# Expert weights of a routed layer streamed in chunks of 2 MB through eight slots, in place of 4 MB through four

## The reference, cut to what matters

```
# hierarchical_moe: h [256, 1024]; 8 groups of 8 experts, FF = 512
g_w, g_idx = top_k(softmax(h @ w_group + b_group), 1)
e_w, e_idx = top_k(softmax(logits of the chosen group), 2)      # weights normalised, times g_w
for each token and each of its two experts e:
    hid = silu(h @ w1[e]) * (h @ w3[e])                         # [512]
    y  += weight * (hid @ w2[e])                                # [1024]
x = x + y
```

## Time and profile before

| | |
|---|---|
| median of 3 runs | 1761.36 us (1760.98 to 1761.41) |
| the profiled execution | 1762.46 us, span 1760.6 us |
| TensorE matmul busy | 1384.9 us (79%) |
| VectorE, ScalarE busy | 19%, 12% |
| DMA queue of SyncE | 503.69 MB, 24080 packets |
| stage of the experts | about 440 to 1348 us of the span |

### The profile page before, as it was taken

The page is one execution under the profiler, slowest core; times in us unless marked ns, Lnnn a source line. Parts: engine busy times, 40 slices in busy tenths (PEclk is TensorE's granted clock), DMA queues, the critical chain, the costliest instruction groups (busy, mean ns, idle before and its releaser), DMA issues.

```text
span 1760.6 us, 16409 instructions
## 1 busy us (share of the span) xinstructions
PE 1384.9 (79%) x7184; PEld 778.7 (44%) x7184; DVE 329.5 (19%) x585; ACT 209.0 (12%) x366; POOL 1.4 (0%) x6
## 2 busy tenths in 40 slices
PE   6999989888866676656666666666667999999996
PEld 5756886775322122212221222122214546788882
DVE  2233432312211001101010101010101221252221
ACT  1000032202000000000000000000001001143300
POOL 0000000000000000000000000000000000000000
PEclk9999998988987788878887888888878999999998
DMA  7324133317999999999999999999997433332310
GB/s 285 114 103 172 67 117 146 102 51 330 394 429 433 433 431 429 433 434 432 429 430 435 433 429 430 435 433 430 430 435 337 171 134 137 132 144 108 142 50 24
DMA packets 24550, 504.43 MB, mean 287 GB/s; under 512 B 4672, under 2 KB 4928, under 8 KB 6336
## 3 DMA queue, kind: packets, MB, share of 16 engines
q1 hardware_dynamic: 24080, 503.69, 68.6%
q10 hardware_dynamic: 432, 0.17, 0.0%
HBM read 502.81 MB, written 1.05 MB: 286 GB/s over the span
## 4 chain that ended last, share of the span: by engine, by line
PE 51%; DMA 44%; DVE 3%; ACT 1%; issue 1%; SPq 0%; DVEq 0%; ACTq 0%
DMA arena<-in_experts 44%; PE psP L803 35%; PE psP L481 5%; PE psP L492 3%; DVE arena L1298 2%; PE psB L1064 1%; PE psB L793 1%; PE psA L948 1%; PE psB L948 1%; PE psA L1030 1%; PE psA L1029 1%; PE psA L793 0%; PE psA L502 0%; PE psP L848 0%; PE psP L842 0%
## 5 line engine op out<-in xcount | busy, mean ns | idle before, releaser
L803 PE MATMUL psP<-arena,ring 128*128 128x256 f32 x1664 | 369.3, 384 | 2.2 <-DVE arena L1298 1.4
L803 PEld LDWEIGHTS psP<-arena,ring 128*128 128x128 f32 x1664 | 319.1, 193 | 48.1 <-issue 4.2
L481 PE MATMUL psP<-ring,arena 128*32 128x512 f32 x1024 | 162.1, 792 | 103.9 <-DMA ring<-in_experts 103.9
L803 PE MATMUL psP<-ring,arena 128*128 128x512 f32 (+2 forms) x576 | 233.1, 564 | 7.3 <-DVE arena L1298 7.3
L481 PE MATMUL psP<-arena 128*32 128x512 f32 x1024 | 158.1, 774 | 99.8 <-DMA arena<-in_experts 99.8
L1298 DVE TENSOR_TENSOR X<-X,psA 128x512 f32<-128x512 f32 x68 | 46.8, 688 | 682.1 <-PE psA L502 682.1
L803 PEld LDWEIGHTS psP<-ring,arena 128*128 128x128 f32 x576 | 105.7, 191 | 126.1 <-issue 126.0
L481 PEld LDWEIGHTS psP<-ring,arena 128*32 128x32 f32 x1024 | 41.0, 139 | 223.2 <-issue 176.5
L481 PEld LDWEIGHTS psP<-arena 128*32 128x32 f32 x1024 | 37.3, 136 | 217.9 <-DMA arena<-in_experts 126.5
L492 PE MATMUL psP<-arena 128*32 128x512 f32 x512 | 76.8, 754 | 53.6 <-DMA arena<-in_experts 49.8
L492 PE MATMUL psP<-ring,arena 128*32 128x512 f32 x512 | 73.4, 725 | 48.0 <-DMA ring<-in_experts 44.5
(11 more groups left out here) (223 smaller groups left out, 748.3 us busy)
## 6 DMA issues: line engine op xcount, KB each, us to landing
arena<-in_experts SPq DMA_DIRECT2D x48, 4096.0 KB, 33.3
ring<-in_experts SPq DMA_DIRECT2D x48, 4096.0 KB, 33.3
ring<-in_u_gl SPq DMA_DIRECT2D x6, 2048.0 KB, 7.7
ring<-in_u_hf SPq DMA_DIRECT2D x2, 2048.0 KB, 11.9
ring<-in_u_hq SPq DMA_DIRECT2D x2, 2048.0 KB, 22.0
ring<-in_u_hv SPq DMA_DIRECT2D x2, 2048.0 KB, 7.7
ring<-in_u_hg SPq DMA_DIRECT2D x2, 2048.0 KB, 7.4
ring<-in_u_ga SPq DMA_DIRECT2D x2, 2048.0 KB, 7.5
```

Source lines behind the costliest of these rows:

```text
L481: mm = pe.matmul(z[j * CAP:(j + 1) * CAP, :], x[:, 4 * half + k, j * CAP:(j + 1) * CAP], held[c % 4][:, j, k * 512:(k + 1) * 512], start=( ...
L803: mm = pe.matmul(dst, lhs_of(o, k), rhs_of(o, k), start=(k == 0), stop=(k == kc - 1))
```

## The change

Chunks are halved: 12 a group, each of 2 MB, each partition's row 16 KB, and eight places in `held`. `used` counts 12 a group. The order in which the first eight places are filled follows a list of their own: after the step wa1 has been read out (areas 8 and 9), after the third product with v (areas 2 and 3), after wb0 (ring slot 3), wb1 (areas 4 and 5, ring slot 0), wo0 (slot 1) and wo1 (slot 2, areas 6 and 7). `wrow` no longer waits for wb1 but for vm1, an earlier step. `up` takes the quarters it is to work as arguments and waits for each; the number and the order of the products, the scatters and the gathers stay as they were. The waits of the second layer's first four units are adapted to the new places.

```diff
-CHUNKS_G = [("w1", 0), ("w1", 1), ("w3", 0), ("w3", 1), ("w2", 0), ("w2", 1)]
+CHUNKS_G = [(w, q) for w in ("w1", "w3", "w2") for q in range(4)]
 NC_G = len(CHUNKS_G)
+HELD = 8
...
-        held = [area(2, EG, 2048), ring[:, 0:2, :].rearrange("p a (h n) -> p (a h) n", h=2),
-                ring[:, 2:4, :].rearrange("p a (h n) -> p (a h) n", h=2), area(6, EG, 2048)]
+        held = [area(8, EG, 1024), area(2, EG, 1024), ring[:, 3, :].rearrange("p (h n) -> p h n", h=EG), area(4, EG, 1024),
+                ring[:, 0, :].rearrange("p (h n) -> p h n", h=EG), ring[:, 1, :].rearrange("p (h n) -> p h n", h=EG),
+                ring[:, 2, :].rearrange("p (h n) -> p h n", h=EG), area(6, EG, 1024)]
...
-            def up(pair, c, z, x, half):
-
-                wait_chunk(pair, c)
-                for k in range(4):
-                    for j in range(EG):
-                        mm = pe.matmul(z[j * CAP:(j + 1) * CAP, :], x[:, 4 * half + k, j * CAP:(j + 1) * CAP],
-                                       held[c % 4][:, j, k * 512:(k + 1) * 512],
-                                       start=(half == 0 and k == 0), stop=(half == 1 and k == 3))
-                mm.then_inc(used, 1)
+            def up(pair, c, z, x, *parts):
+
+                for q in parts:
+                    wait_chunk(pair, c + q)
+                    for k in range(2):
+                        for j in range(EG):
+                            mm = pe.matmul(z[j * CAP:(j + 1) * CAP, :], x[:, 2 * q + k, j * CAP:(j + 1) * CAP],
+                                           held[(c + q) % HELD][:, j, k * 512:(k + 1) * 512],
+                                           start=(q == 0 and k == 0), stop=(q == 3 and k == 1))
+                    mm.then_inc(used, 1)
...
-            wait_full(sp, ("proj", "wb1"))
+            wait_full(sp, ("proj", "vm1"))
             sp.dma_start(wrow, ins["final_norm_w"].unsqueeze(0).broadcast_to([P, D])).then_inc(row_in, 16)
...
-            before_chunk = [("proj", "wb1"), ("proj", "wo0"), ("proj", "wo1"), ("proj", "wo1")]
+            freed_by = [(empty, "wa1"), (full, "pv"), (full, "wb0"), (full, "wb1"), (full, "wb1"), (full, "wo0"), (full, "wo1"),
+                        (full, "wo1")]
...
-                        sp.wait_ge(used, r * (GROUPS * NC_G) + q * (2 * NC_G) + (c - 3))
+                        sp.wait_ge(used, r * (GROUPS * NC_G) + q * (2 * NC_G) + (c - (HELD - 1)))
...
-                    sp.wait_ge(used, rounds * (GROUPS * NC_G) - (2 if n < 2 else 1))
+                    sp.wait_ge(used, rounds * (GROUPS * NC_G) - (3, 2, 1, 5)[n])
...
-    stream = np.empty((GROUPS, NC_G, P, EG, 2048), np.float32)
+    stream = np.empty((GROUPS, NC_G, P, EG, 1024), np.float32)
```

More of the change, by code:

```diff
@@ L383, in build @@
         rounds_ready = sem("rounds_ready")
-        chunk_in = [sem(f"chunk_in_{i}") for i in range(4)]
+        chunk_in = [sem(f"chunk_in_{i}") for i in range(HELD)]
         used = sem("used")
@@ L452, in chunk_of @@
         def chunk_of(c):
-            return held[c % 4], chunk_in[c % 4]
+            return held[c % HELD], chunk_in[c % HELD]
         SCATTER = [(0, 0, 0), (0, 1, 512), (1, 0, 0), (1, 1, 512)]
@@ L472, in wait_chunk, with down @@
             def wait_chunk(pair, c):
-                pe.wait_ge(chunk_in[c % 4], pair * 48 + 16 * (c // 4 + 1))
-            def up(pair, c, z, x, half):
-                wait_chunk(pair, c)
-                for k in range(4):
-                    for j in range(EG):
-                        mm = pe.matmul(z[j * CAP:(j + 1) * CAP, :], x[:, 4 * half + k, j * CAP:(j + 1) * CAP],
-                                       held[c % 4][:, j, k * 512:(k + 1) * 512],
-                                       start=(half == 0 and k == 0), stop=(half == 1 and k == 3))
-                mm.then_inc(used, 1)
-            def down(pair, c, half):
-                wait_chunk(pair, c)
-                for f in range(2):
+                pe.wait_ge(chunk_in[c % HELD], pair * 48 + 16 * (c // HELD + 1))
+            def up(pair, c, z, x, *parts):
[7 more added lines that the diff above has]
+                    mm.then_inc(used, 1)
+            def down(pair, c):
+                for f in range(4):
+                    wait_chunk(pair, c + f)
                     for cols in range(2):
@@ L492, in down @@
                             mm = pe.matmul(zY[j * CAP:(j + 1) * CAP, cols * 512:(cols + 1) * 512],
[L493 to L496, removed]
+                                           hidT[:, f, j * CAP:(j + 1) * CAP],
+                                           held[(c + f) % HELD][:, j, cols * 512:(cols + 1) * 512],
+                                           start=(f == 0), stop=(f == 3))
+                    mm.then_inc(used, 1)
             def scatter(parts):
@@ L522, in moe_tensor @@
                         pe.wait_ge(gate_read, it + 1)
-                        up(pair, c, zG, xs[u], 0)
+                        up(pair, c, zG, xs[u], 0, 1)
                         pe.wait_ge(xs_ready, it * 2 + 2)
@@ L528, in moe_tensor @@
                         scatter((0, 1))
-                        up(pair, c + 1, zG, xs[u], 1)
+                        up(pair, c, zG, xs[u], 2, 3)
                         pe.wait_ge(hid_ready, it + 1)
-                        up(pair, c + 2, zU, xs[u], 0)
+                        up(pair, c + 4, zU, xs[u], 0, 1)
                         pe.wait_ge(added, it * 4 + 2)
                         scatter((2, 3))
-                        up(pair, c + 3, zU, xs[u], 1)
+                        up(pair, c + 4, zU, xs[u], 2, 3)
                         pe.wait_ge(sel_ready, it + 2)
@@ L548, in moe_tensor @@
                         pe.wait_ge(hidT_ready, it + 1)
-                        down(pair, c + 4, 0)
-                        down(pair, c + 5, 1)
+                        down(pair, c + 8)
             last = pe.snap(rounds * GROUPS)
@@ L567, in moe_scalar @@
                     it = act.snap(r * GROUPS + g)
-                    act.wait_ge(used, it * NC_G + 2)
+                    act.wait_ge(used, it * NC_G + 4)
                     act.wait_ge(hid_ready, it + 1)
@@ L575, in moe_scalar @@
                     act.activation(hidT.rearrange("p f n -> p (f n)"), ps["B"][:, 0:512], ACT.Copy).then_inc(hidT_ready, 1)
-                    act.wait_ge(used, it * NC_G + 6)
+                    act.wait_ge(used, it * NC_G + 12)
                     act.wait_ge(scattered, it * 4 + 4)
@@ L695, in experts @@
                         add(it, 2, 3)
-                        dve.wait_ge(used, it * NC_G + 4)
+                        dve.wait_ge(used, it * NC_G + 8)
                         dve.wait_ge(gate_read, it + 2)
@@ L738, in _ @@
             sp.dma_start(rtw[:, :, 8:72], ins["router_expert_w"][0].rearrange("(k p) n -> p k n", p=P)).then_inc(rt_in, 16)
-            wait_full(sp, ("proj", "wb1"))
+            wait_full(sp, ("proj", "vm1"))
             sp.dma_start(wrow, ins["final_norm_w"].unsqueeze(0).broadcast_to([P, D])).then_inc(row_in, 16)
-            before_chunk = [("proj", "wb1"), ("proj", "wo0"), ("proj", "wo1"), ("proj", "wo1")]
+            freed_by = [(empty, "wa1"), (full, "pv"), (full, "wb0"), (full, "wb1"), (full, "wb1"), (full, "wo0"), (full, "wo1"),
+                        (full, "wo1")]
             def pair_loads(r, q, peeled):
                 for c in range(2 * NC_G):
-                    if peeled and c < 4:
-                        wait_full(sp, before_chunk[c])
+                    if peeled and c < HELD:
+                        sems, step = freed_by[c]
+                        for region, n in USE[("pv", 2) if step == "pv" else ("proj", step)].items():
+                            sp.wait_ge(sems[region], n)
                     else:
-                        sp.wait_ge(used, r * (GROUPS * NC_G) + q * (2 * NC_G) + (c - 3))
+                        sp.wait_ge(used, r * (GROUPS * NC_G) + q * (2 * NC_G) + (c - (HELD - 1)))
                     src = ins["experts"][c] if peeled else ins["experts"][bass.ds(q * (2 * NC_G) + c, 1)].rearrange("a p n -> p (a n)")
-                    sp.dma_start(held[c % 4].rearrange("p e n -> p (e n)"), src).then_inc(chunk_in[c % 4], 16)
+                    sp.dma_start(held[c % HELD].rearrange("p e n -> p (e n)"), src).then_inc(chunk_in[c % HELD], 16)
             pair_loads(0, 0, True)
@@ L1716, in laid_out @@
     given["consts"] = shape_constants()
-    stream = np.empty((GROUPS, NC_G, P, EG, 2048), np.float32)
[L1719 to L1724, removed]
+    stream = np.empty((GROUPS, NC_G, P, EG, 1024), np.float32)
+    for c, (which, q) in enumerate(CHUNKS_G):
+        rows = 1 if which == "w2" else 2
+        w = np.asarray(inputs[f"expert_{which}"])[0].reshape(GROUPS, EG, 4 * rows, P, -1)
+        w = w[:, :, q * rows:(q + 1) * rows].transpose(0, 1, 3, 2, 4)
+        stream[:, c] = w.reshape(GROUPS, EG, P, 1024).transpose(0, 2, 1, 3)
+    given["experts"] = stream.reshape(GROUPS * NC_G, P, EG * 1024)
     return given
```

## The result

The changed kernel takes 1765.36 us (median of 20 runs, 1759.77 to 1769.32) against 1761.11 (20 runs, 1759.29 to 1762.14) for the kernel before: ratio **1.0023**, 95% interval 1.0014 to 1.0031. It is slower by 4 us, where 1.2 us faster was forecast. The profiled execution took 1765.40 us, span 1763.6. Two executions of the whole study, one of long_end (2760 us) and one of the kernel before (3903 us), took far longer than all others and are left out of the ratios.

What follows compares the result with a forecast made beforehand. The prediction took the DMA stream of the experts' weights as the bound between 440 and 1354 us. First refill -1.8 - 0.4, rate +2.9 and end -1.9 made -1.2 us: 1760.2 us for the median, range 1755.0 to 1765.6.

Steps and rivals of the forecast that it cites:

- What bounds the kernel: Experts' stage: DMA loads set the time, 9.718 us per 4 MB; outside 440 to 1354 us TensorE does.
- First fills: Ahead of the experts' stage: issuing the first chunks earlier only moves idle DMA time about, 0 us.
- First refill: Front of the stream: refill issued after 16 products, not 32, -1.8 us; shorter time from issue to effect, -0.4.
- The rate: Middle of the stream: 184 refills of 2 MB replace 92 of 4 MB, costing 0 to 8.3 us, taken as +2.9.
- Its own sign of being wrong: Stream: the forecast is wrong if the period of landings is off 4.875 us by more than 0.02.
- The end: Last landing to xk's projection, 11.85 us: only 16 products remain, clock rising early in the scatter, -1.9 us.
- three cases: End: all at full clock -4.3 us; last chunk at half -2.6; chunk, scatters and xk's start at half +2.9.
- Behind 1354 us: After the experts' stage: TensorE sets the time and the change touches nothing there.
- The sum: Whole kernel: -1.8 - 0.4 + 2.9 - 1.9 = -1.2 us.
- Rival 2: Middle of the stream: each transfer costs something of its own on the DMA engines, +4.2 to +6.1 us; chance 0.11.
- Rival 3: Experts' stage: finer bursts hold TensorE's clock down, about +13 us, 1774; chance 0.04.

Runs made afterwards that it cites:

- long_end: Changed kernel, but in down TensorE waits for the third and fourth chunk together, so the last burst is 32 products: ratio 1.0031, repeated 1.0029.
- late_fills: Changed kernel, but the first three chunks and wrow are issued only when wb1 has ended, as before the change: ratio 1.0021 to the kernel before.
- before_again: The kernel before, unchanged, profiled once more: profiled execution 1761.45 us.
- after_fourth: The changed kernel, unchanged, in its fourth profile: profiled execution 1768.22 us, with 12.91 us from the last landing to xk's projection.
- rows16: Kernel before, still 96 loads of 4 MB, but each partition's 32 KB brought as two rows of 16 KB: ratio 1.0043.
- two_loads: Kernel before, each 4 MB chunk brought by two 2 MB loads with rows of 16 KB, TensorE waiting for both: ratio 1.0039.
- paired: Changed kernel with 4 MB loads in the old places, only chunks 4 and 11 (of 0 to 11) split in two: 1756.37 us, ratio 0.9977.
- after_warm: Changed kernel with three unread 128x512 products added behind the second and behind the third chunk of down: 1762.88 us, ratio 1.0012.
- rows8: Kernel before, still loads of 4 MB, but each partition's 32 KB brought as four rows of 8 KB: ratio 1.0115.

## Why the prediction was wrong

**What bounds the kernel** was right: TensorE waits for DMA in every group, the first layer didn't move (the first product stands at 440.03, before at 440.50), and `down` waits for three of its four chunks. One reading was off, without weight: 19 slices, not 20, have 429 to 435 GB/s.

**First fills: 0.** Right, by late_fills.

**First refill: -1.8 - 0.4.** The issue is 1.7 us sooner against the first product. But the first sixteen together are only 0.8 us ahead: chunk 23 is started 84.40 us after the first product, the same bytes (chunk 11) 85.19 before; 16 x 0.039 of that is the rate, so -1.4 was gained at the front, not -2.2. Why not more isn't shown.

**The rate: +2.9.** This is the step that failed. The price was taken as 0.016 us per transfer from seven loads, whose rounding allowed up to 0.045. It is 4.898 - 4.859 = 0.039: 184 x 0.039 = 7.2 us. Seven loads with landing times to a tenth of a microsecond can't tell 0.016 from 0.039; the text said so, and still forecast the value that the loads happened to give. Its own sign of being wrong, a period over 0.02 off 4.875, is met (4.898). The three row lengths measured here give what carries the price: without any rows 4 MB would take 9.718 - 8 x 0.0096 = 9.641 us, 435.0 GB/s, and each engine pays 9.6 ns a row on top.

The Trainium skill, DMA: Bandwidth & Descriptors, "Where 436 GB/s comes from", has 435.2 GB/s as the ceiling, and by it 4 MB would take an estimated 9.638 us; the 9.641 above agrees. With this figure the 9.718 of the kernel before could have been read: if its missing 0.080 us per 4 MB were put down to the 8 rows of each engine, 8 more would cost as much again, 92 x 0.080 = 7.4 us in place of 2.9. In the Trainium skill, DMA: Bandwidth & Descriptors, "Why small descriptors are slow" gives three cycles of overhead per packet, by the 850 MHz that the page has for the fabric an estimated 3.5 ns; here a row costs 9.6 ns, and the measurement decides.

**The end: -1.9.** It was named as three cases, and it comes as the first of them, all at full clock, in four of five profiles with the changed kernel's end (-4.1, the changed kernel's four and late_fills) and near the third in one (+1.1). The forecast had the clock rise only early in the scatter; in the four it is up from the first of the last 16 products. Why it is one or the other isn't shown.

**Behind 1354 us: nothing.** The prediction let the change touch nothing there. The order of work didn't change, but layer 2 took 408.5, 404.9, 404.9 and 406.8 us in the changed kernel's four profiles, and 406.7 and 406.8 in the two of before. This was a term of its own, of either sign.

**The sum** for the usual kind of stage: first refill -1.4, rate +7.2, end -4.1, together +1.7; the table has 915.06 - 913.39 = +1.67. The timed medians differ by 4.2. The profiled execution of the changed kernel (1765.40) lies at its median, and before_again (1761.45) lies close to that of before: of their 3.95 us, 1.85 are the stage, 1.75 layer 2 and 0.30 the time ahead of the first product. In after_fourth the end has the loss instead. So what goes beyond the 1.7 is the clock in the profiles, at the end or in layer 2; how the 2.5 us of the medians divide between the two stays open. Rival 2 (slower by a cost of its own per transfer) was right in its place and near in its size, wrong in its carrier: the row pays, not the load. That its sum for the rounding's upper end, +4.2, equals the difference of the medians is luck: its parts were -2.2, +8.3 and -1.9. Rival 3 (the finer bursts hold the clock down) was right in that bursts of 16 products can have a price at the end (after_fourth), wrong in that the whole stage would slow: its mean clock is 0.85, before it was 0.82. The measured time lies 0.2 us below the upper end of the range.

**Still open.** Why the runs of before, rows16 and two_loads lie within 3.5 us (the last two with 4 runs each) and those of the changed kernel, late_fills, paired and long_end within 6 to 10. Part of it is the end; another part is layer 2, 406.6 to 406.8 us in all five profiles of kernels in which TensorE works through 4 MB at a time, 403.5 to 410.0 in the others. Its differences are time at half clock, as shown above, but what sets how often the clock falls there is open: neither the length of the last burst nor its clock explains it.

## What to carry to other kernels

Where a stage runs at the rate of the DMA engines, the number of rows that each engine moves is a term of its own: keep rows as long as the places allow, and if finer grain is wanted, get it from semaphores and counting, with the small loads only where they shorten a wait on the path (here 2 of 12, 4.9 us faster than before by the medians, where all of them small was 4 slower). A price per transfer that is to be multiplied by 184 must be known to a hundredth of a microsecond, which takes long stretches under wait, not a handful of landings. A short burst of products that ends a DMA-bound stage may run at half clock, together with what follows it; cheap products in the waits ahead of it kept the last two bursts at full clock in the two profiles that have them, and in after_warm none of 11 runs was over 1765 us. And one profile of each kernel isn't enough for differences of some us: the same program's second layer differed by 3.6 us between two executions.

## What the runs showed of the hardware

A row of 8, 16 or 32 KB costs each DMA engine 9.6 ns beside its bytes, with 435.0 GB/s for all 16 as the rate extrapolated to no rows (9.718, 9.795 and 9.949 us for 4 MB in before, rows16 and rows8); a second load in the queue costs 0.004 us (two_loads). The granted clock can stay at 0.50 while TensorE is busy 7.4 of 9.4 us (above). It can also fall in the middle of projections; TensorE stretches of the changed kernel:

```profile
1525.00:1530.00 5.00, 4.58 (x24) 3.87 (x25) 2.69 (x4) 1.64 (x3) 0.00 (x0) 0.73 0.90 374
```

From shortly after 1527 to 1530 TensorE is busy all the time, at 0.50, and the chain's piece there takes 15.70 us where it takes 14.01 in the kernel before. This is the step by which layer 2 took 408.5 us in this profile and 406.7 before. In the 9.1 us ahead of the fall (1518.0 to 1527.1) TensorE was idle for 1.27 us in all, and the kernel before has the same pause of 1.27 us at this place and no fall behind it.
